# Attention scores as fp32r matmuls of the full array, with high and low parts of Q and K, in a YOCO decoder step

## The reference

```python
k = rope_partial((kv_in @ w_k).reshape(bsz, seqlen, N_HEADS, 2, HEAD_DIM), pos)
q = rope_partial((h @ w_q).reshape(bsz, seqlen, N_HEADS, 2, HEAD_DIM), pos)
s = einsum("bqhcd,bkhcd->bhcqk", q, k) * HEAD_DIM ** -0.5      # HEAD_DIM = 64
s = where(k_pos <= q_pos, s, -1e30)
p = softmax(s, axis=-1)
w = p[:, :, 0] - lam * p[:, :, 1]                              # differential attention
o = einsum("bhqk,bkhe->bqhe", w, v)
```

## Time and profile before

| | us |
|---|---|
| three runs, median | 2425.14 (2422.55 to 2428.04) |
| profiled execution, span from its first to its last instruction | 2420.9 |
| TensorE (PE) busy | 2349.3 (97%) |
| VectorE (DVE) busy | 1508.1 (62%) |
| GpSimd (POOL) busy | 843.5 (35%) |
| ScalarE (ACT) busy | 750.4 (31%) |

### The profile page before, as it was taken

The page is one execution under the profiler, slowest core; times in us unless marked ns, Lnnn a source line. Parts: engine busy times, 40 slices in busy tenths (PEclk is TensorE's granted clock), DMA queues, the critical chain, the costliest instruction groups (busy, mean ns, idle before and its releaser), DMA issues.

```text
span 2420.9 us, 40635 instructions
## 1 busy us (share of the span) xinstructions
PE 2349.3 (97%) x16326; PEld 2276.2 (94%) x16326; DVE 1508.1 (62%) x2499; ACT 750.4 (31%) x1440; POOL 843.5 (35%) x557
## 2 busy tenths in 40 slices
PE   7899999999999999999999999999999999999998
PEld 6889999999999999999999766699999999999997
DVE  9993257555555576775534577756755555557766
ACT  4452134333333211031100377843433333320103
POOL 0003325544445443332332000043555444443431
PEclk9899999999999999999999999999999999999999
DMA  3155101222222422212256454210222222242212
GB/s 123 38 141 175 53 18 66 82 70 73 71 79 79 166 85 90 88 53 88 88 184 209 126 145 141 71 36 18 70 79 79 79 79 71 70 157 105 79 62 71
DMA packets 107540, 221.41 MB, mean 91 GB/s; under 512 B 35802, under 2 KB 59866, under 8 KB 107362
## 3 DMA queue, kind: packets, MB, share of 16 engines
q1 hardware_dynamic: 94130, 179.95, 23.3%
q10 hardware_dynamic: 13232, 38.94, 4.4%
HBM read 171.79 MB, written 44.71 MB: 89 GB/s over the span
## 4 chain that ended last, share of the span: by engine, by line
PE 84%; DVE 11%; issue 2%; ACT 1%; DMA 1%; POOL 0%; SPq 0%; DVEq 0%; ACTq 0%; POOLq 0%
PE pair L2130 45%; PE pair L2384 12%; PE pair L2387 12%; PE pair L2388 12%; PE pair L2617 1%; DVE nmx L1933 1%; DVE act_lo L1454 1%; DVE Vp L1373 1%; DMA zn<-zblk 1%; DVE wmix L2010 1%; DVE acc L1373 1%; DVE Vp L1795 1%; PE pair L2298 1%; DVE act_lo L1407 0%; DVE G_im L1373 0%
## 5 line engine op out<-in xcount | busy, mean ns | idle before, releaser
L2384 PE MATMUL pair<-act_hi,w_hi 128*128 128x344 f32 x1408 | 450.0, 320 | 6.7 <-DVE gate L1373 3.0
L2388 PE MATMUL pair<-act_hi,w_lo 128*128 128x344 f32 x1408 | 450.1, 320 | 0.0
L2387 PE MATMUL pair<-act_lo,w_hi 128*128 128x344 f32 x1408 | 449.9, 320 | 0.0
L2130 PE MATMUL pair<-act_hi,w_hi 128*128 128x344 f32 x1152 | 371.1, 322 | 2.7 <-DVE act_lo L1373 2.1
L2130 PE MATMUL pair<-act_hi,w_lo 128*128 128x344 f32 x1152 | 368.2, 320 | 0.0
L2130 PE MATMUL pair<-act_lo,w_hi 128*128 128x344 f32 x1152 | 368.0, 319 | 0.0
L732 POOL CAST w_hi<-w_raw 128x1024 fp32r<-128x1024 f32 x90 | 114.8, 1276 | 722.8 <-issue 309.5
L1373 DVE TENSOR_TENSOR X<-X,pair 128x344 f32<-128x344 f32 x528 | 252.9, 507 | 150.8 <-PE pair L2130 150.8
L2130 PE MATMUL pair<-hid_hi,w_hi 128*128 128x344 f32 x1056 | 338.2, 320 | 1.1 <-POOL w_lo L735 1.1
L2130 PE MATMUL pair<-hid_lo,w_hi 128*128 128x344 f32 x1056 | 338.5, 321 | 0.0
L2130 PE MATMUL pair<-hid_hi,w_lo 128*128 128x344 f32 x1056 | 338.0, 320 | 0.0
(11 more groups left out here) (308 smaller groups left out, 4199.7 us busy)
## 6 DMA issues: line engine op xcount, KB each, us to landing
w_raw<-w SPq DMA_DIRECT2D x180, 512.0 KB, 4.0
hid_raw<-hid SPq DMA_DIRECT2D x20, 1032.0 KB, 5.7
hid<-gate ACTq DMA_DIRECT2D x22, 516.0 KB, 2.7
hid<-gate_odd ACTq DMA_DIRECT2D x22, 516.0 KB, 2.6
kpg<-cache_k SPq DMA_DIRECT2D x16, 512.0 KB, 5.4
vpg<-cache_v SPq DMA_DIRECT2D x16, 512.0 KB, 7.0
qd<-qt SPq DMA_DIRECT2D x28, 256.0 KB, 5.4
ublk<-x_b SPq DMA_DIRECT2D x8, 576.0 KB, 8.3
```

Of the source, the lines that this page charges most:

```text
L2130: return t_.matmul(out, lhsT, rhs, start=start, stop=stop)
L2384: ins = t_.matmul(out, wh, rhs[k][0], start=first and k == 0, stop=False, skip_group_check=True)
L2387: t_.matmul(out, wh, rhs[k][1], start=False, stop=False, skip_group_check=True)
L2388: last = t_.matmul(out, wl, rhs[k][0], start=False, stop=k == HK - 1, skip_group_check=True)
```

## The change

- The scores of a half x become fp32r matmuls of the full array. The keys' high part (rounded to fp32r) stands on rows 0 to 63 and their low part (the rest) on rows 64 to 127; the queries' high part, twice on the rows, is the weight of a first matmul, their low part of a second one. Both go over up to 512 keys at a time; one bf16 matmul of 128 columns adds the mask.
- The parts are made beside the projections: ACT makes the high part of each Q and K tile (16 in all), POOL the low part, ACT stores both to a new DRAM array `qk`. There are two buffers for high parts and one for low parts. `qt` is gone.
- A head's loads are 13 DMAs: 4 for keys, 8 for queries, 1 for values. The second head's keys are loaded after the last projection is evicted.
- The row maximum and the exponential read the scores as one run of columns. Two semaphores are merged with others, and the program reserves less SBUF for DMA descriptors.

```diff
+SPLIT_ORDER = (2, 3, 0, 1) + tuple(range(4, 2 * KT))
+HEAD_IN = 208
...
+        hq = place("hq", [P, 3, SEQ], F32R)
...
+        kh = [place("kh0", [P, 2, SEQ], F32R, rg),
+              nc.alloc_sbuf_tensor_at("kh1", [P, 2, SEQ], F32R, offset=RAW_AT + 16384)]
...
@@ SP: loads of a head @@
+                high, low = into or qh[par], (ql1[0], ql1[1]) if par else (ql0[:, 0], ql0[:, 1])
+                for c in range(2):
+                    for l, out in enumerate((high[:, 1 - c, :], low[1 - c])):
+                        for g in range(2):
+                            sp.dma_start(out[64 * g:64 * g + 64, :].bitcast(F32), d["qk"][0, l, 2 * h + c].rearrange("m j t -> (m j) t")
+                                         ).then_inc(hd_in[par], 16)
...
+                for c in range(2):
+                    for l in range(2):
+                        sp.dma_start(kh[par][64 * l:64 * l + 64, 1 - c, :].bitcast(F32), d["qk"][1, l, 2 * h + c].rearrange("m j t -> (m j) t")
                                      ).then_inc(hd_in[par], 16)
...
-            sp.wait_ge(rope_out, 64)
+            sp.wait_ge(rope_out, 32)
+            sp.wait_ge(hl_out, 32 * len(SPLIT_ORDER))
...
             load_keys(6)
-            load_key_rows(1, 1)
             load_keys(NS - 1)
...
             sp.wait_ge(kv_evicted, 6 * 3 * KT // 2)
+            load_key_rows(1, 1)
             load_queries(1, 1)
@@ POOL @@
+            def low_of_rows(i):
+                pool.wait_ge(hl_hi, i + 1)
+                if i:
+                    pool.wait_ge(hl_out, 32 * i)
+                g.tensor_tensor(hq[:, 2, :], rows_in_turn(i), hq[:, i % 2, :].bitcast(F32), ALU.subtract).then_inc(hl_lo, 1)
...
-            split_units(U_DOWN[0] + 4, SEG1, 1)
+            split_units(U_DOWN[0] + 4, U_KVQ - 2, 1)
+            for u in range(U_KVQ - 2, SEG1, 2):
+                split_one(u, 1)
+                split_one(u + 1, 1)
+                for i in {3: (0, 1, 2, 3), 4: (4, 5), 5: (6, 7), 6: (8, 9), 7: (10, 11), 8: (12, 13), 9: (14, 15)}.get((u - U_KVQ) // 2, ()):
+                    low_of_rows(i)
@@ ACT @@
+            def store_split(i):
+                tt = SPLIT_ORDER[i]
+                act.wait_ge(hl_lo, i + 1)
+                for l, x in enumerate((i % 2, 2)):
+                    act.dma_start(rows_of(d["qk"][tt // KT, l])[tt % KT], hq[:, x, :].bitcast(F32)).then_inc(hl_out, 16)
+
+            def high_of_rows(i):
+                if i >= 2:
+                    act.wait_ge(hl_out, 32 * (i - 1))
+                a.activation(hq[:, i % 2, :], rows_in_turn(i), ACT.Copy).then_inc(hl_hi, 1)
+                if i:
+                    store_split(i - 1)
...
                 if not rot:
                     act.wait_ge(kv_evicted, max(6 * (tt // 2) + 6, 12))
-                    act.dma_start(which[m], stage[:, slot, :]).then_inc(kv_out[slot], 16)
+                    if tt >= KT:
+                        act.dma_start(which[m], stage[:, slot, :]).then_inc(kv_out[slot], 16)
+                    if tt < 2 * KT:
+                        high_of_rows(SPLIT_ORDER.index(tt))
...
+                if tt in (3, KT + 1):
                     act.wait_ge(kv_roped, 1 + tt // KT)
                     for x in range(2):
+                        high_of_rows(SPLIT_ORDER.index(tt // KT * KT + x))
+                if tt == 2 * KT - 1:
+                    store_split(2 * KT - 1)
...
-                    a.activation(by_key(prob[:, v % 2, x, 0:2 * w]), by_bank(pair[x][:], w), ACT.Exp, bias=nmx[:, v % 2, x:x + 1],
+                    a.activation(prob[:, v % 2, x, 0:n], pair[x][:, 0:n], ACT.Exp, bias=nmx[:, v % 2, x:x + 1],
@@ DVE @@
+                    if kvq_tile - 3 < 2 * KT and not slots[kvq_tile - 3][1]:
+                        dve.wait_ge(hl_lo, SPLIT_ORDER.index(kvq_tile - 3) + 1)
...
-                    dve.wait_ge(rope_out, 32 * (kvq_tile // KT))
+                    if kvq_tile > KT:
+                        dve.wait_ge(hl_lo, SPLIT_ORDER.index(1) + 1)
@@ TensorE: scores(v, x) @@
-                w = (i + 1) * 64
-                for g in range(2):
-                    rows = slice(64 * g, 64 * g + 64)
-                    mm(bank[2 * x + g][:, 0:w], (qd[par] if h else qd_first)[rows, x, i * P:(i + 1) * P], kh[rows, par, x, 0:w], True, False)
-                for g in range(2):
-                    rows = slice(64 * g, 64 * g + 64)
-                    last = mm(bank[2 * x + g][:, w - 64:w], identb[rows, :], maskb[rows, :], False, True)
-                last.then_inc(a_s, 1)
+                q = slice(i * P, (i + 1) * P)
+                high = (qh[par] if h else qh_first)[:, x, q]
+                low = ql1[x][:, q] if par else ql0[:, x, q]
+                for k0 in range(0, (i + 1) * P, SEQ // 2):
+                    ks = slice(k0, min(k0 + SEQ // 2, (i + 1) * P))
+                    final = ks.stop < (i + 1) * P
+                    mm(pair[x][:, ks], high, kh[par][:, x, ks], True, False)
+                    mm(pair[x][:, ks], low, kh[par][:, x, ks], False, final)
+                mm(pair[x][:, q], identb[:], maskb[:], False, True).then_inc(a_s, 1)
```

More of the change, by code:

```diff
@@ L140, in build @@
         identb = place("identb", [P, P], BF16)
-        maskb = place("maskb", [P, 64], BF16)
+        maskb = place("maskb", [P, P], BF16)
         ones = place("ones", [P, P], F32)
@@ L277, in build @@
         rf = [ACT_AT, HID_AT]
-        qd1 = place("qd1", [P, 2, SEQ], F32, rf)
+        qh1 = place("qh1", [P, 2, SEQ], F32R, rf)
         vT = nc.alloc_sbuf_tensor_at("vT", [P, 2, SEQ], F32, offset=RAW_AT)
@@ L294, in build @@
         rg = [MISC_AT, END]
[L295 to L297 removed]
+        kh = [place("kh0", [P, 2, SEQ], F32R, rg),
+              nc.alloc_sbuf_tensor_at("kh1", [P, 2, SEQ], F32R, offset=RAW_AT + 16384)]
+        qh = [place("qh0", [P, 2, SEQ], F32R, rg), qh1]
+        qh_first = nc.alloc_sbuf_tensor_at("qh_first", [P, 2, SEQ], F32R, offset=HID_AT + 4 * T * 4)
+        ql0 = nc.alloc_sbuf_tensor_at("ql0", [P, 2, SEQ], F32R, offset=HQ_AT)
         rg[0] = MISC_AT + 3 * CW * 4 * 2 + T * 4 + DM * 4
@@ L306, in build @@
         oS2 = place("oS2", [P, NS, NH], F32, rg)
+        QROW_AT = rg[0]
         qrow = place("qrow", [NS, HC, 8, 8], F32, rg)
+        ql1 = [nc.alloc_sbuf_tensor_at(f"ql1{x}", [P, SEQ], F32R, offset=at)
+               for x, at in enumerate((HQ_AT + 2 * SEQ * 4, QROW_AT))]
         orow = stok[:].rearrange("p j s -> p (j s)")
@@ L317, in build @@
         blk_in = sem("blk_in")
-        x_in = [sem(f"x_in{n}") for n in range(NC)]
+        x_in = sem("x_in")
         w_in = [sem(f"w_in{r}") for r in range(4)]
@@ L378, in build, with rows_in_turn @@
         slots = [(tt % 4, tt in (0, 1, KT, KT + 1)) for tt in range(3 * KT)]
-        n_out = [16 * sum(1 for s, r in slots if s == x and not r) for x in range(4)]
-        n_qk = [16 * sum(1 for s, r in slots[:2 * KT] if s == x and not r) for x in range(4)]
+        n_out = [16 * sum(1 for s, r in slots[KT:] if s == x and not r) for x in range(4)]
+        n_qk = [16 * sum(1 for s, r in slots[KT:2 * KT] if s == x and not r) for x in range(4)]
         def bc(ap, axis, shape):
             return ap.unsqueeze(axis).to_broadcast(shape)
[L385 to L389, removed]
+        def rows_in_turn(i):
+            tt = SPLIT_ORDER[i]
+            slot, rot = slots[tt]
+            return roped[:, tt % KT, 0:SEQ] if rot else stage[:, slot, 0:SEQ]
         def by_step(ap):
@@ L1904, in _ @@
             c.step(v_.tensor_scalar(ngain[:], gains[:, 2:4, :], -1.0, None, ALU.mult))
-            for n in range(NC):
-                dve.wait_ge(x_in[n], 16)
+            dve.wait_ge(x_in, 16 * NC)
             with dve.Fori(0, KT - 2) as m:
@@ L1956, in _ @@
                 slot = slots[kvq_tile][0]
-                if not slots[kvq_tile][1]:
+                if kvq_tile >= KT and not slots[kvq_tile][1]:
                     seen[slot] += 16
@@ L2763, in constants @@
     tok = order[:P]
[L2764 to L2774, removed]
+    masked = np.where(tok[None, :] > tok[:, None], f(-1e30), f(0))
     nvec = np.concatenate([np.arange(NW), L * np.arange(NJ), L * NJ * np.arange(NI)]).astype(f)
@@ L2870 @@
             "ssm_s": (P, 2, PAIRS, NS)}
-    scratch = {"z": (PARTS, L, 16, GP, NB), "zn": (PARTS, 16, GP, NS), "qt": (HC, KT, 8, T), "qrow": (NS, DM),
+    scratch = {"z": (PARTS, L, 16, GP, NB), "zn": (PARTS, 16, GP, NS), "qrow": (NS, DM),
                "hid": (FT, P, T)}
-    nc = bacc.Bacc("TRN2", target_bir_lowering=False, num_devices=1)
+    nc = bacc.Bacc("TRN2", target_bir_lowering=False, num_devices=1, dynamic_dma_scratch_size=1024)
     d = {"n_pages": arrays["cache_k"].shape[0]}
```

50 lines of the change are left out of this document (21 added, 29 removed).

## The result

The changed kernel takes 2438.20 us at the median of 8 runs (2430.38 to 2444.16), the kernel before, on the same chips, 2424.45 (8 runs): ratio 1.0052, 95% interval 1.0037 to 1.0068. It is slower by 0.5%, where 2419.9 was forecast. The profiled execution has a span of 2439.0 us, 18.1 more than the one before.

A forecast was written before the change was run, and what follows sets the result against it. TensorE, busy 97% of the span, was taken as the bound, DVE and ACT in the score loop. Span 2420.9 - 6.4 (attention) + 1.2 (stall) = 2415.7; with 4.2 from span to median, 2419.9 us; range 2414.5 to 2427.

The forecast's parts named there:

- Scores on TensorE: Attention, score blocks as full-array fp32r matmuls plus a mask matmul: -0.34 us a head.
- the way in: Attention, entry into the half-array form costs 0.09 us and goes; five entries in the TensorE-bound part: -0.45 us a head.
- H at pair 3: Projections, pair 3 to 4: time from issuing a part's two stores to both landed, taken as 5.0 us, between 4.5 and 6.8.
- Each microsecond of H above 5 costs three: Start of pair 4: three landings stand in the chain, so each extra microsecond of store-and-landing time adds three.
- DVE beside POOL: Start of pair 4: eight low parts of activations take 6.41 us beside POOL, 2.4 more than ACT needs; stall +1.2 us.
- Later pairs have room: Projections after pair 4: POOL needs 17.5 us of the 22.6 that a pair's matmuls take.
- rival 1: Projections, one-buffer hand-over: landing time above 7.1 us makes the stall at pair 4 exceed the gain; 2428.5 us, chance 0.12.
- Behind which only DVE's key products stand: Projections, sampled-query row on ACT slips by up to 8 us; only DVE's key products wait, once every 15 us for 5.
- Loads of a head: Attention, 13 DMAs instead of 9, 5.5 MB with cache values; cover 3 to 5 us, so cost nothing.
- merged semaphores: Merged semaphores and smaller scratch touch no wait that ends late: nothing.
- Rivals 2 and 4: Attention; 2: gain waited away in the loop, 2425.5 us, chance 0.09; 4: full-array weight loads stand bare, 2472, chance 0.02.
- rival 3: Attention, a head's loads at 220 GB/s come 1 us late in four heads: +4, 2424 us, chance 0.05.

The follow-up runs named there:

- two_low: The changed kernel with a second buffer for low parts, subtraction i waiting for the stores of i-2: 2419.69 us, ratio 0.9982 to the kernel before.
- highs_early: The changed kernel with ACT making the high parts of the K/V activations ahead of high part 5 and the store of part 4: 2430.66 us, ratio 1.0026.
- no_keys: The changed kernel without the loads of cached keys after the first pair of pages: 2426.58 us, ratio 1.0011 to the kernel before.
- last_key: The changed kernel with DVE's last sampled-token key products behind the eviction that the first scores wait for: 2432.20 us, ratio 1.0041.
- qrow_first: The changed kernel with ACT copying and storing the sampled-query row right behind its wait for the rotated K: 2435.47 us, ratio 1.0043.

## Why the prediction was wrong, by its steps

*Scores on TensorE, and the way in: right.* Forecast -0.79 us for a head of the middle. The head from 1454.34 to 1482.75 takes 28.41 against 29.37: -0.91 in the TensorE-bound part (14.21 against 15.12), +0.12 in the loop-bound one (11.70 against 11.58), -0.17 in the last step. 512 columns come at 0.230 (forecast 0.227). A block of four takes 1.22 (forecast 1.13), the way in gives 0.17 (forecast 0.09): one sum, cut at another place, because the extra 0.09 lies behind the first matmul's start and so counts into the block. Over eight heads the attention gives 6.5 us in the profile of the changed kernel and 4.5 to 5.7 in the nine profiles of the experiments. What is missing to 8 x 0.96 lies in heads 1 and 6: behind pauses of 1.8 and 2.1 us, which the kernel before has too (1.8 and 1.9), the clock falls in six and in nine of the ten profiles, and not before. Two windows of two_low and of before, head 1:

```profile
1393.00:1399.00 6.00, 5.62 (x22) 4.42 (x23) 3.86 (x6) 4.43 (x12) 0.00 (x0) 0.72 1.03 231
```

```profile
1388.70:1394.70 6.00, 5.23 (x34) 2.80 (x35) 4.82 (x7) 4.34 (x12) 0.00 (x0) 1.00 1.01 297
```

What makes the difference between the two forms was not tried. For want of this the forecast of -6.4 was 1 to 2 us too good in most runs; that the profile of the changed kernel shows 6.5 is the luck of a clock that fell only once in it.

*H at pair 3: right in size.* I took H = 5.0 and a period of 7.5; the first subtractions come 7.85 apart, so H is 5.45. "Each microsecond of H above 5 costs three" put the high parts at 1170.3 then; they begin at 1173.28, of which 2.6 is the late start of this execution. The stop of 2.1 us at pair 4 is what this step gives (forecast 1.2).

*DVE beside POOL: mis-sized.* The prediction knew that eight low parts of activations take 6.41 us beside POOL, and used it for one chunk. Pushed back, the second chunk falls on subtraction 5 and POOL's splits of weights behind it:

```profile
1173.90 3.99 DVE L1450 SCALAR_TENSOR_TENSOR act_lo<-X,gains,act_hi 128x344 fp32r<-128x344 f32 x8 [11.88 <-ACT act_hi L902]
...
1178.66 11.08 DVE L1450 SCALAR_TENSOR_TENSOR act_lo<-X,gains,act_hi 128x344 fp32r<-128x344 f32 x8
```

11.1 us instead of 4 made the second stop, 4.2 us and 1.6 of half clock; POOL's own instructions fill 9.0 of the 11.1. The Trainium skill ("SBUF — State Buffer", Who interferes with whom) says that a DVE instruction with two SBUF inputs contends with a GpSimd instruction that reads SBUF, and this trace agrees: an `act_lo` has two. In highs_early the slow chunk is the first (10.6 us from 1164.84), nine us earlier than here, and neither stop is there.

*"Later pairs have room": the step that failed.* It priced a pair at 7.5 + 2.5 + H + 2.5 = 17.5 of 22.6 us: with one landing, and with the H of pair 3, before the key loads begin. Both were wrong. The DMA issues of 1128 to 1180 us, and below of 1230 to 1330 us (count, KB each, median us to landing), give another H from there on:

```profile
qk<-hq ACTq DMA_DIRECT2D x10, 512.0 KB, 4.4
```

```profile
qk<-hq ACTq DMA_DIRECT2D x16, 512.0 KB, 6.7
kpg<-cache_k SPq DMA_DIRECT2D x10, 512.0 KB, 7.0
```

Ahead of subtractions 13 and 15 POOL waits 9.9 and 10.4 us. At H = 10.4 the prediction's own sum for a pair is 22.9, and the room is gone.

The second landing comes from the order on ACT: the stores of part i-1 are issued behind high part i (`high_of_rows`), and that waits for its own tile. Subtraction 7 ends at 1206.3, but its stores go out at 1221.6, behind the rotation of K, and subtraction 8 waits 15.0 us:

```profile
1203.87 2.40 POOL L800 TENSOR_TENSOR hq<-stage,hq 128x1024 fp32r<-128x1024 f32 x1 [5.43 <-DMA qk<-hq]
1221.61 2.98 ACTq L1260 DMA_DIRECT2D qk<-hq  x2
1230.13 2.39 POOL L800 TENSOR_TENSOR hq<-roped,hq 128x1024 fp32r<-128x1024 f32 x1 [14.98 <-DMA qk<-hq]
```

Behind it stand POOL's splits, behind these SP's weight units and the first cached keys (17 us later than before), behind these DVE's first products, and behind these the eviction of the last chunk of pair 6. ACT's next high part and the stores of part 11 wait for that eviction, and POOL for the stores:

```profile
1259.54 2.85 DVE L1416 TENSOR_TENSOR kpg<-kpg,qb 128x1024 f32<-128x1024 f32 x1 [13.32 <-DMA kpg<-cache_k]
1268.13 0.93 DVE L1620 SCALAR_TENSOR_TENSOR stage<-pair,R 128x344 f32<-128x344 f32 x2
1269.69 1.06 ACT L1266 ACTIVATE hq<-stage 128x1024 fp32r<-128x1024 f32 x1 [22.10 <-DVE stage L1620]
```

From there two slow landings, two subtractions and the split of two units end at 1303.9, 4.6 us after TensorE wanted them. The three late stops and the half clock behind them are 15.7 us, those of pair 4 7.9 (forecast for all: 1.2). This is rival 1's mechanism (chance 0.12) with its bound of H > 7.1 passed, not at pair 4, where I placed it, but from pair 8 on. In no_keys, with the first keys as late (DVE waits 12.5 us for them) but with waits of 5.7 and 5.4 us ahead of subtractions 13 and 15, the late stops vanish; two_low takes the landing out of POOL's order and they vanish but for one. How much of each late stop is slow landing and how much is the order no run separates: issuing the stores of a part right behind its subtraction was not tried.

*"Behind which only DVE's key products stand": wrong.* The row slipped by 18 us, where 8 were forecast. On DVE the evictions stand behind the key products. Eight rounds of one key buffer (product, load, landing) fill the stage: the last load came at 1331 before and at 1361 after, and its product held up the eviction that the first scores wait for, 4.4 us and 2.8 at half clock. last_key shows the order, qrow_first that the row was not what delayed the loads.

*The clock: not priced.* Rivals and range counted stops only. Here each microsecond of the three long stops cost half a microsecond more (6.9 for 13.2).

*Loads of a head, merged semaphores: right.* TensorE waits for no head's loads but the first V rows, which show only once the eviction is out of the way. Rivals 2 and 4 are out by the attention's own numbers, rival 3 too.

## What to carry to other kernels

A store behind which an engine must wait costs its landing each time, at the landing time of the busiest stretch, not of the quiet one in which it can be read: before a hand-over goes into an engine's order, list what else that engine feeds (here POOL's splits, then SP's loads, then DVE's products, then evictions) and price each with the slow landing. The same holds for a store that is issued behind the next piece of work: it waits for that work's input too. A second buffer of 4 KB per partition turned 0.5% slower into 0.2% faster, and moving one product behind the eviction that the next stage waits for added 0.1%, which the overlapping intervals (0.9971 to 0.9993, 0.9962 to 0.9983) do not quite tell. Here each of the three stops of over 4 us cost 6 to 7 with the clock behind it.

## What the runs showed of the hardware

- The granted clock stood at 0.50 to 0.52 for 3 to 6 us behind each of the three stops of 4.2 to 4.6 us in the changed kernel. It stayed at 1.00 behind its stops of 2.1 and 1.4 us and behind those of 1.7 us in last_key and no_keys (up to 1175.4 and 1175.8), but not behind one of 2.2 us in highs_early (mean 0.70 over 5.7 us).
- An fp32r matmul with 128-column weights starts 0.230 us behind the last for 512 columns; behind a bf16 or fp32 matmul the first one takes 0.09 more, in every half.
- DVE's 128x344 low parts take 0.50 us each alone and 1.39 beside POOL's subtraction and splits.
- The wait for two 512 KB stores is 5.4 us at pair 3, where only weight units load beside them, and 9.9 and 10.4 us beside loads of cached keys, with 243 GB/s on the core's queues between 1230 and 1330 us.
